# Expert gathers of six token tiles as one sequence, with layer 1's attention laid beside them

## The chip, the core and the metric

The kernel runs on one core of a Trainium2 chip, as a single launch. The metric is the device time of the launch in microseconds, as the median of several runs; lower is better. The engines are TensorE (PE, with its weight loads PEld), VectorE (DVE), ScalarE (ACT), GpSimd (POOL) and SyncE (SP). SP and POOL issue the transfers (DMA), each in a queue of its own. Engines work in parallel, each in its own order, and wait for each other with semaphores.

## What is computed

One inference step of two layers over 384 tokens (256 prompt frames and 8 streams of 16 frames), 1024 features each, all in fp32. The 384 tokens are three tiles of 128. Layer 0 is an RWKV-7 time mixing, layer 1 a differential attention; each is followed by a PEER mixer of 8 heads that picks 16 of 16384 experts per head and token. Cut to that mixer and the order of things:

```python
s = einsum('nhcd,ckd->nhck', q, sub_keys)           # q = xr @ w_query
s1, i1 = top_k(s[:, :, 0], 16); s2, i2 = top_k(s[:, :, 1], 16)
top_s, top_pos = top_k(all sums s1 + s2, 16)        # 256 candidates a head
gate = softmax(top_s); u = expert_u[eidx]
h = gelu(einsum('nhkd,nd->nhk', u, xr))
out = einsum('nhk,nhkd->nd', gate * h, expert_v[eidx])
...
x = layer_norm(DN_ALPHA * x + mix); x = layer_norm(DN_ALPHA * x + peer_ffn(x))
```

So every token needs 128 rows of expert_u and expert_v, 1 MB for each of the 128 slots of a tile of 128 tokens, 128 gathers per tile and 768 in all. Keys and values of layer 1 come from x after layer 0; the prompt's tokens see the tokens of their own and earlier chunks of 64, the sample tokens their stream's cache of 512 and their own 16.

## The kernel before

The program is a row of stages, each an `nc.Block()` at whose end all engines meet. Within a layer the stages hold all three tiles. In order: the RWKV projections, time mixing per tile, output projection and norm; `peer(0)`; `attention`; `peer(1)`; `store_rows`.

`peer` turns x to features, computes the key scores of tile 0 alone (`first_scores`) and then runs `peer_experts`. There VectorE first chooses the experts of tile 0 (`choose`, top 16 of 16 score rows and of 8 candidate rows), while TensorE and ScalarE compute the key scores of tiles 1 and 2 (`KeyScores`, weights in a ring of two 1 MB buffers). POOL then issues one gather per slot: row `expert[:, t, s]` of `in_peer_uv` for each of the 128 tokens (one per partition), 8 KB per row, u and v side by side, into a ring of ten buffers, `pair_ring`. For each gather VectorE makes the dot product of u and x (`L1386`); for two of them ScalarE applies gelu (`L1410`) and VectorE the gate (`L1392`), ScalarE writes the product on a diagonal (`L1415`), and TensorE multiplies diagonal and v into `pacc`, 128 columns of weights by two halves of 512 (`L1436`, fp32, two passes each). Its end frees the buffer (`row_used`) and lets POOL issue the gather ten further on. The choice for the next tile and the norm of the last one are laid between the dots by hand (`side`). The two layers' gathers are two separate loops of 384.

`attention` projects K, V and Q for all tiles (weights read once through `aw_ring`), turns them, runs the prompt's heads (`prompt_attention`, one step per head with both prompt tiles), the sample streams (`sample_attention`, one step per stream; the cached keys are turned on TensorE, `L1744`), the norm per head and the output projection. No gather runs there.

Of the kernel before, what the change touches and what calls it, by code (L numbers as in the profile page):

```python
# [19 lines left out]
P = 128  # L20
D = 1024
# [13 lines left out]
SLOTS = PH * PTOP  # L35
ALPHA = (2.0 * 2) ** 0.25
# [6 lines left out]
def constant_layout():  # L43

    widths = [("ident", P), ("strict_incl", 2 * P), ("lower", P), ("block", P), ("chunk", NCH), ("first", NCH),
              ("causal", 3 * P), ("pair_ident", N), ("map0", 1), ("map1", 1), ("sum_maps", DD), ("iota", PTOP), ("cos", TILES * ROT // 2),
# [8 lines left out]
def shape_constants():  # L55
# [16 lines left out]
    put("pair_ident", row % N == np.arange(N)[None, :])  # L72

# [37 lines left out]
class Core:  # L111

    def __init__(self, nc, ctx):
        self.nc, self.ctx = nc, ctx
        self.signals = {}

    def sig(self, name):
        if name not in self.signals:
            self.signals[name] = Signal(self.ctx, self.nc, name)  # L120
        return self.signals[name]

# [964 lines left out]
class KeyScores:  # L1087

    HC = 2 * PH
    PAIR = 2 * P

    def __init__(self, core, io, ctx, xT, scores, layer, tiles, ring):
        def sb(name, shape, dt=F32):
            return ctx.enter_context(core.nc.sbuf_tensor(f"{name}_{layer}_{tiles[0]}", shape, dt))

        self.core, self.io, self.xT, self.scores, self.layer, self.tiles, self.ring = core, io, xT, scores, layer, tiles, ring  # L1100
        self.rows = slice(tiles[0] * P, (tiles[-1] + 1) * P)
        self.width = len(tiles) * P
        self.wq = sb("wq", [P, ring, KD, self.PAIR])
        self.keys, self.keysT = sb("keys", [P, 2, P]), sb("keysT", [P, 2, P])
        self.qT = sb("qT", [P, self.HC, self.width])
        self.bank = [ctx.enter_context(core.nc.psum_tensor(f"pbank{i}_{layer}_{tiles[0]}", [P, HALF], F32)) for i in range(6)]
        self.wq_in = [core.sig(f"loaded{i}") for i in range(ring)]
        self.keys_in, self.keys_psum, self.keys_done = core.sig(f"loaded{ring}"), core.sig("keysT_psum"), core.sig("keys_done")
        self.q_psum, self.q_done = core.sig("rows_psum"), core.sig("rows_copied")
        self.s_psum, self.s_done = core.sig("s_psum"), core.sig("ps_done")  # L1110

    def loads(self, sp):
        sp.dma_start(self.keys[:], self.io["peer_sub_keys"][self.layer].rearrange("c k d -> k c d")).then_inc(*self.keys_in.by(16))
        for i in range(PH):
            if i >= self.ring:
                sp.wait_ge(*self.q_psum.at(2 * (i - self.ring) + 2))
# [1008 lines left out]
```

## Time and profile before

| | us |
|---|---|
| median of 3 runs | 3494.87 |
| lowest, highest | 3494.45, 3506.02 |
| the profiled execution, its own time | 3500.28 |
| its span in the trace | 3498.5 |
| TensorE, VectorE, ScalarE, POOL busy | 2615.5, 1768.4, 659.7, 946.1 |
| HBM read, written | 938.81 MB, 18.12 MB |

The profile is of one execution. Busy times are of the span, the weight loads of TensorE (1419.4 us) lie beside its products. A share of DMA is the mean over the core's 16 DMA engines. The first gather is issued at 960.69 us, layer 0's last norm is done near 1952, and layer 1's gathers run from about 2500 to 3478.5.

### The profile page before, as it was taken

To read this page: it belongs to the slowest core of one execution; us is meant where nothing else is said; L and a number is where in the kernel's file an instruction comes from. 1 tells how busy PE (TensorE), PEld (TensorE's weight loads), DVE (VectorE), ACT (ScalarE), POOL (GpSimd) and SP (SyncE) were. 2 spreads that over 40 slices of the span, in tenths; PEclk is the share of its full clock that TensorE was granted. 3 is DMA by queue.
4 is the path that set the end of the run, shared out by engine and by line. 5 is a ranking of instruction groups with operands and counts; after the bars stand their busy time and mean duration, and the time that the engine had idled before them with its cause. 6 is when DMAs were issued, how large, how long until landed. Compare 5 with 4: busy or idle time off the path is not lost. (4 is left out here: it accounts for less than half of the span.)

```text
span 3498.5 us, 32692 instructions
## 1 busy us (share of the span) xinstructions
PE 2615.5 (75%) x11853; PEld 1419.4 (41%) x11853; DVE 1768.4 (51%) x4015; ACT 659.7 (19%) x1800; POOL 946.1 (27%) x929
## 2 busy tenths in 40 slices
PE   7949494866977777777777794887877777777776
PEld 3427383753842322232222343666733222322222
DVE  1133534322558657855555204432778567755555
ACT  0022121220121211122112103311111211121112
POOL 0013130310044433444434000000144434443332
PEclk9979696987999999999999895988999999999999
DMA  5220204023599999999999412523699999999997
GB/s 176 86 107 2 73 1 100 1 44 131 164 391 420 420 420 420 403 420 420 420 420 420 160 66 120 223 103 101 242 416 412 420 420 420 407 420 420 420 420 319
DMA packets 193198, 959.04 MB, mean 274 GB/s; under 512 B 33232, under 2 KB 67200, under 8 KB 94736
## 3 DMA queue, kind: packets, MB, share of 16 engines
q0 software_dynamic: 114784, 821.12, 56.9%
q1 hardware_dynamic: 78256, 135.84, 11.6%
q8 instruction: 96, 1.57, 0.2%
q14 instruction: 62, 0.51, 0.0%
HBM read 938.81 MB, written 18.12 MB: 274 GB/s over the span
## 5 line engine op out<-in xcount | busy, mean ns | idle before, releaser
L1436 PE MATMUL pacc<-pair_ring,diag 128*128 128x512 f32 x3072 | 1439.5, 615 | 489.0 <-ACT diag L1415 488.9
L1289 POOL DMA_INDIRECT pair_ring<-in_peer_uv,expert x768 | 800.9, 1043 | 1679.4 <-PE pacc L1436 1089.6
L1386 DVE CUSTOM_DVE_ANT_0 pair_ring<-pair_ring,x_tok 128x1024 f32<-128x1024 f32 x768 | 939.5, 1225 | 622.5 <-DMA pair_ring<-in_peer_uv,expert 619.5
L1436 PEld LDWEIGHTS pacc<-pair_ring,diag 128*128 128x128 f32 x3072 | 571.2, 195 | 1356.0 <-issue 1344.6
L1410 ACT ACTIVATE acts<-dots 128x2 f32<-128x2 f32 x384 | 78.1, 203 | 1384.3 <-DVE dots L1386 1384.0
L1415 ACT ACTIVATE diag<-constants_sb,mix 128x128 f32<-128x128 f32 x768 | 266.2, 393 | 145.0 <-DVE mix L1392 143.2
L1130 PE MATMUL pbank<-peer_xT,wq 128*128 128x128 f32 (+1 forms) x1024 | 178.3, 340 | 14.0 <-DMA wq<-in_peer_w_query 14.0
L1130 PEld LDWEIGHTS pbank<-peer_xT,wq 128*128 128x128 f32 x1024 | 162.9, 201 | 29.5 <-DMA wq<-in_peer_w_query 15.3
L275 PE MATMUL acc<-w_ring,mixed 128*128 128x512 f32 x288 | 125.8, 599 | 10.0 <-issue 9.1
L1487 PE MATMUL aacc<-aw_ring,at_xT 128*128 128x512 f32 x288 | 126.4, 601 | 6.2 <-DMA aw_ring<-in_w_kv 5.6
L1392 DVE TENSOR_TENSOR mix<-gate,acts 128x2 f32<-128x2 f32 x384 | 59.6, 155 | 68.0 <-ACT acts L1410 68.0
L720 DVE TENSOR_TENSOR x<-bank,x 128x512 f32<-128x512 f32 x48 | 33.2, 692 | 116.1 <-PE bank L578 116.1
L275 PEld LDWEIGHTS acc<-w_ring,mixed 128*128 128x128 f32 x288 | 55.1, 192 | 80.0 <-issue 80.0
L1487 PEld LDWEIGHTS aacc<-aw_ring,at_xT 128*128 128x128 f32 x288 | 55.3, 193 | 76.8 <-issue 70.4
L339 DVE SCALAR_TENSOR_TENSOR mixed<-dxT,mu_cols,xT 128x384 f32<-128x384 f32 x48 | 25.8, 612 | 114.3 <-PEq L284 114.2
L517 PE MATMUL bank<-constants_sb,wkv_a 128*128 128x128 f32 x24 | 8.0, 334 | 81.9 <-PEq L382 79.9
L1195 DVE MAX8 best<-scores 128x8 f32<-128x128 f32 x96 | 21.8, 281 | 87.3 <-PEq L1160 87.3
L1386 DVE DVE_READ_ACCUMULATOR2_ANT dots<- 128x1 f32 x768 | 63.5, 83 | 0.0
L525 PE MATMUL bank<-own_ar,feat 128*128 128x256 f32 x192 | 51.8, 430 | 14.9 <-ACT own_ar L673 14.9
L769 POOL TENSOR_TENSOR B_by_chunk<-wkv_B_end,constants_sb 128x512 f32<-128x512 f32 x48 | 50.0, 1042 | 42.3 <-PE bank L610 42.2
L760 POOL MEMSET own_ar<- 128x1024 f32 x3 | 2.9, 952 | 216.2 <-POOLq L382 216.2
L416 PE MATMUL run<-wkv_z,constants_sb 128*128 128x512 f32 x12 | 11.3, 1100 | 59.3 <-DVEq L424 59.3
(372 smaller groups left out, 2639.1 us busy)
## 6 DMA issues: line engine op xcount, KB each, us to landing
wq<-in_peer_w_query SPq DMA_DIRECT2D x32, 1024.0 KB, 5.9
cache_k<-in_cache_k SPq DMA_DIRECT2D x8, 2048.0 KB, 12.2
cache_v<-in_cache_v SPq DMA_DIRECT2D x8, 2048.0 KB, 8.7
w_ring<-in_rwkv_w_rkv SPq DMA_DIRECT2D x24, 512.0 KB, 3.3
pair_ring<-in_peer_uv,expert POOLq DMA_INDIRECT x768, 18.4
aw_ring<-in_w_kv SPq DMA_DIRECT2D x16, 512.0 KB, 8.6
pn_w_rwkv<-in_rwkv_w_out SPq DMA_DIRECT2D x8, 512.0 KB, 7.1
aw_ring<-in_diff_w_q SPq DMA_DIRECT2D x8, 512.0 KB, 3.2
```

Source lines behind the costliest of these rows:

```text
L275: mm = pe.matmul(acc[:, 2 * t + h, :], xm[:, k, t * P:(t + 1) * P], w_ring[:, n % RING, h * HALF:(h + 1) * HALF], start=(k == 0), stop=(k ...
L525: mm = pe.matmul(bank[first + q][:, r * 2 * P:(r + 1) * 2 * P], feat[:, g % 2, q, n, :], own_ar[:, h].rearrange("k i t -> k (i t)"))
L720: dve.tensor_tensor(x[:, g % 2, (i + 1) % 2], quad(bank[4 + i % 2], P), x[:, g % 2, i % 2], ALU.add).then_inc(*x_done.by())
L769: pool.tensor_tensor(dst[:, h], src[:, head(g, h)].unsqueeze(1).broadcast_to([P, NCH, N]), spread, ALU.mult).then_inc(*exp_done.by())
L1130: mm = pe.matmul(self.bank[m % 3][:, 0:self.width], self.wq[:, m // 2 % self.ring, k, (m % 2) * P:(m % 2 + 1) * P], self.xT[:, k, self.row ...
L1289: pool.indirect_dma_start(ring[:, g % RING, :], None, io["peer_uv"], bass.IndirectOffsetOnAxis(ap=expert[:, t, s:s + 1], axis=0)).then_inc ...
L1386: dve.tensor_tensor_reduce(ring[:, g % RING, 0:D], ring[:, g % RING, 0:D], x[:, t, :], 1.0, 0.0, ALU.mult, ALU.add, dots[:, t % 2, s:s + 1 ...
L1392: dve.tensor_tensor(mix[:, t % 2, now], gate[:, t % 2, now], acts[:, t % 2, now], ALU.mult).then_inc(*mix_done.by())
L1410: act.activation(acts[:, t % 2, now], dots[:, t % 2, now], ACT.Gelu).then_inc(*gelu_done.by())
L1415: act.activation(diag[:, (g + j) % DIAGS, :], core.const("ident"), ACT.Copy, scale=mix[:, t % 2, i * BATCH + j:i * BATCH + j + 1]).then_in ...
L1436: mm = pe.matmul(acc[:, half, :], diag[:, g % DIAGS, :], ring[:, g % RING, D + half * HALF:D + (half + 1) * HALF], start=(s == 0), stop=(s ...
L1487: mm = pe.matmul(acc[:, b, :], xT[:, k, t * P:(t + 1) * P], ring[:, n % RING, h * HALF:(h + 1) * HALF], start=(k == 0), stop=(k == KD - 1))
```

## The change

The gathers of both layers become one sequence of 384 turns of two gathers, kept by a class `Flow` whose counters and buffers live over the whole program. A stage gets a number of ticks and the turn at which it must have arrived (`plan`), and calls `flow.vector`, `flow.scalar`, `flow.tensor` and `flow.gpsimd` after each tick of its own work; they carry the turns up to `due(n)`, TensorE and POOL one tick behind. Layer 1 is now worked through tile by tile (`attention_tile`): norm of the expert output of the tile, features, K/V/Q projection, features of K and Q, attention (tiles 0 and 1 of the prompt, tile 2 the sample streams), norm per head, output projection, features, key scores. The weights for these are read again for each tile. Its 27 stages carry turns 66 to 262, then `run_flow` and `ffn_norm` carry the rest.

A gather now serves 64 tokens, each with two of its slots: partition w and w + 64 both belong to token w. The expert numbers and gates of a tile go to DRAM and come back in that order (`turn_rows_out`, `turn_rows_in`), x is copied in it (`spread_rows`), all on POOL's queue. Two gathers j = 0, 1 serve the two halves of the tokens; each multiplies with 64 columns of weights, at columns 0 and 64 of the array. Number of gathers and their bytes stay as they were. The lambda stage (`mixing_weight`) moves ahead of the first experts, the gather buffers serve as weight ring for layer 0's key scores, and the caches come in another layout from the host, so that cached keys are no longer turned on the chip.

```diff
+class Flow:
+    RING, DIAGS = 10, 3
...
+    def due(self, n):
+        return self.first + (self.last - self.first) * n // self.ticks
...
+    def tensor(self, pe, n):
+        while self.summed < self.due(n - 1):
+            u, q = divmod(self.summed, TURNS)
+            if q == 0 and u > 0:
+                pe.wait_ge(*self.ffn_done.at(u))
+            for half in range(2):
+                for j in range(GROUPS):
+                    g = self.summed * GROUPS + j
+                    if half == 0:
+                        pe.wait_ge(*self.landed(g))
+                        pe.wait_ge(*self.diag_done.at(g + 1))
+                    mm = pe.matmul(self.acc[j * FOLD:(j + 1) * FOLD, half, :], self.diag[:, self.summed % self.DIAGS, j, :],
+                                   self.ring[:, g % self.RING, D + half * HALF:D + (half + 1) * HALF],
+                                   start=(q == 0), stop=(q == TURNS - 1), tile_position=(0, j * FOLD))
...
+    def gpsimd(self, pool, n):
...
+        while self.gathered < min(self.due(n - 1) * GROUPS + self.RING, self.known * SLOTS):
+            u, s = divmod(self.gathered, SLOTS)
+            q, j = divmod(s, GROUPS)
+            if s == 0:
+                pool.wait_ge(*self.turn_in.at(32 * GROUPS * (u + 1)))
+            if self.gathered >= self.RING:
+                pool.wait_ge(*self.row_used.at(self.gathered - self.RING + 1))
+            pool.indirect_dma_start(self.ring[:, self.gathered % self.RING, :], None, self.io["peer_uv"],
...
+    def turn_rows_out(self, pool, u):
+        pool.wait_ge(*self.soft_done.at(u + 1))
+        pool.dma_start(self.core.turn_at[u], self.expert[:]).then_inc(*self.turn_out.by(16))
+        pool.dma_start(self.core.turn_gate[u], self.gate[:]).then_inc(*self.turn_out.by(16))
+    def turn_rows_in(self, pool, u):
+        pool.wait_ge(*self.turn_out.at(32 * (u + 1)))
...
-            for s in range(SLOTS):
-                        for half in range(2):
-                            mm = pe.matmul(acc[:, half, :], diag[:, g % DIAGS, :], ring[:, g % RING, D + half * HALF:D + (half + 1) * HALF],
-                                           start=(s == 0), stop=(s == SLOTS - 1))
-                        mm.then_inc(*row_used.by())
...
-        peer(core, io, 0)
-        attention(core, io)
-        peer(core, io, 1)
-        store_rows(core, io)
...
+        open_flow(core, io, flow, xT, choice)
+        attention_tile(core, io, flow, 0, neg_lam, kT, v_tok, [
+            (69, dict(turn=((2, 0, 3),), rows=((2, 1),))), (71, {}), (86, {}), (90, {}), (102, {}), (106, {}), (115, {}), (118, {}), (130, {})])
+        attention_tile(core, io, flow, 1, neg_lam, kT, v_tok, [
+            (133, dict(rows=((3, 1),))), (135, {}), (152, dict(u=3, side=75)), (156, dict(side=20)), (168, dict(side=50, end=8)),
+            (171, dict(turn=((3, 1, 0),))), (180, dict(turn=((3, 0, 2),))), (182, {}), (194, {})])
+    attention_tile(core, io, flow, 2, neg_lam, None, None, [
+        (197, dict(rows=((4, 1),))), (199, dict(u=4, side=15)), (216, dict(side=110)), (221, dict(side=25, end=12, turn=((4, 15, 0),))), (240, dict(turn=((4, 0, 4),))),
+        (243, {}), (250, {}), (252, {}), (262, {})])
+    run_flow(core, flow, 32, 294, u=5, side=160, end=28, rows=((5, 1),), turn=((5, 31, 0),))
+    ffn_norm(core, io, flow, 3, 298)
+    run_flow(core, flow, 30, 328, turn=((5, 0, 4),))
+    ffn_norm(core, io, flow, 4, 332)
+    run_flow(core, flow, 52, 384)
+    ffn_norm(core, io, flow, 5, 384)
```

A number in the lists is the turn that the stage ends with; the nine stages of a tile are `ffn_norm`, `turn_features`, `attention_projections`, `turn_features`, the attention, `head_norm`, `project_tile`, `turn_features`, `key_scores`. `u` and `side` start a tile's choice of experts beside the stage and set its steps, `end` the tick at which it is done, `turn` the ticks of the stores and loads of expert numbers, `rows` that of the copies of x.

On POOL's queue the gathers of one layer stood in one run, with the stores of K and V behind them (before):

```order
L1289 DMA pair_ring<-in_peer_uv,expert 128x2048 x384
L1274 UNCONDITIONAL_BRANCH
L1464 UNCONDITIONAL_BRANCH
L1473 DMA out_cache_v_p<-at_v 128x2x1024
L1474 DMA out_cache_v_s<-at_v 128x1024
```

Now, around the head norm of tile 1 and the output projection behind it, the store of expert numbers stands between gathers, and its loads wait for it (after):

```order
L1373 DMA fl_pairs<-in_peer_uv,fl_row_at 128x2048 x22
L1799 UNCONDITIONAL_BRANCH
L2161 UNCONDITIONAL_BRANCH
L1380 DMA turn_at<-fl_expert 128x128
L1381 DMA turn_gate<-fl_gate 128x128
L1373 DMA fl_pairs<-in_peer_uv,fl_row_at 128x2048 x8
L2156 UNCONDITIONAL_BRANCH
L2231 UNCONDITIONAL_BRANCH
L1373 DMA fl_pairs<-in_peer_uv,fl_row_at 128x2048 x2
L1390 DMA fl_row_at<-turn_at 64x2x64 x2
L1390 DMA fl_row_gate<-turn_gate 64x2x64 x2
```

Ten gathers stand between the store and its loads; everything behind the loads on this queue waits for the store to land.

On ScalarE the heads of the prompt attention stood without any expert work between them (before; `pa_p` are the probabilities):

```order
L1637 ACTIVATE pa_p,pa_tot<-pa_s,pa_low 128x128
L1637 ACTIVATE pa_p,pa_tot<-pa_s,pa_low 128x256
L1637 ACTIVATE pa_p,pa_tot<-pa_s,pa_low 128x128
L1637 ACTIVATE pa_p,pa_tot<-pa_s,pa_low 128x256
L1626 COPY pa_attnT<-pa_t 128x384
L1628 COPY at_oT<-pa_o 128x256
```

Now one tick of the stage of tile 0 reads (after; the functions Exp and Gelu lie in different tables):

```order
L1845 ACT_TABLE_LOAD
L1845 ACTIVATE pa_p,pa_tot<-pa_s,pa_low 128x128 x2
L1850 COPY pa_attnT<-pa_t 128x128
L1852 COPY at_oT<-pa_o 128x128
L1317 ACTIVATE fl_diag<-constants_sb,fl_mix 128x64 x2
L1325 ACT_TABLE_LOAD
L1325 ACTIVATE fl_acts<-fl_dots 128x2
```

A diagonal, a gelu and two table loads stand in each head's step.

## Rows read from the trace of the kernel before

In rows of engines' busy time the columns are the stretch, its length, then busy us (and instructions) of PE, PEld, DVE, ACT and POOL, the granted TensorE clock as a share of full speed, the DMA share, and GB/s. Rows in order of time begin with start and duration in us.

**Rows 1.** The page, part 2: the span in 40 slices.

```profile
PEclk9979696987999999999999895988999999999999
DMA  5220204023599999999999412523699999999997
GB/s 176 86 107 2 73 1 100 1 44 131 164 391 420 420 420 420 403 420 420 420 420 420 160 66 120 223 103 101 242 416 412 420 420 420 407 420 420 420 420 319
```

**Rows 2.** Busy time (and instructions) of each engine by stretch.

```profile
960.00:1930.00 970.00, 724.63 (x1626) 296.47 (x1625) 605.89 (x1392) 191.61 (x597) 399.93 (x384) 0.98 1.01 416
...
1957.00:2100.00 143.00, 132.38 (x317) 61.06 (x318) 8.21 (x16) 12.49 (x23) 2.59 (x4) 0.95 0.30 110
...
2108.00:2180.00 72.00, 32.67 (x143) 23.10 (x144) 32.93 (x113) 22.05 (x81) 1.51 (x1) 0.55 0.36 146
2180.00:2320.00 140.00, 120.45 (x1259) 92.63 (x1257) 56.67 (x146) 40.76 (x113) 2.04 (x2) 0.94 0.44 166
2320.00:2345.00 25.00, 18.08 (x96) 17.80 (x96) 13.37 (x39) 1.15 (x2) 0.00 (x0) 0.64 0.08 25
...
2403.00:2447.00 44.00, 36.15 (x290) 35.41 (x290) 0.21 (x2) 6.99 (x21) 0.00 (x0) 0.88 0.62 194
```

**Rows 3.** The same view between the end of one tile and the next.

```profile
1298.79:1623.10 324.31, 240.04 (x512) 95.23 (x512) 220.94 (x537) 63.94 (x200) 137.84 (x128) 0.97 1.01 415
1623.10:1944.24 321.14, 237.88 (x512) 93.33 (x512) 171.40 (x327) 61.05 (x196) 120.17 (x119) 0.99 0.98 406
```

**Rows 4.** The page, part 5: the expert groups.

```profile
L1436 PE MATMUL pacc<-pair_ring,diag 128*128 128x512 f32 x3072 | 1439.5, 615 | 489.0 <-ACT diag L1415 488.9
L1289 POOL DMA_INDIRECT pair_ring<-in_peer_uv,expert x768 | 800.9, 1043 | 1679.4 <-PE pacc L1436 1089.6
L1386 DVE CUSTOM_DVE_ANT_0 pair_ring<-pair_ring,x_tok 128x1024 f32<-128x1024 f32 x768 | 939.5, 1225 | 622.5 <-DMA pair_ring<-in_peer_uv,expert 619.5
```

**Rows 5.** PE in order of time: 64-column stationaries, then 128.

```profile
276.08 1.94 PE L600 MATMUL bank<-B_by_chunk,x 128*64 128x512 f32 x8
...
1019.37 3.67 PE L1436 MATMUL pacc<-pair_ring,diag 128*128 128x512 f32 x8 [1.31 <-ACT diag L1415]
```

**Rows 6.** DMA queues in 20 to 22 us: packets, MB, share of time.

```profile
q1 hardware_dynamic: 108, 0.42, 52.9%
q0 software_dynamic: 111, 0.41, 50.7%
```

**Rows 7.** Queue q1 in 1963:2033, 2108:2320, 2345:2352 and 2403:2447.

```profile
q1 hardware_dynamic: 3312, 12.06, 48.0%
...
q1 hardware_dynamic: 8448, 33.56, 41.3%
...
q1 hardware_dynamic: 752, 2.74, 98.3%
...
q1 hardware_dynamic: 8592, 8.52, 62.0%
```

**Rows 8.** Start of the expert stage in order of time.

```profile
960.69 1.06 POOL L1289 DMA_INDIRECT pair_ring<-in_peer_uv,expert  x1 [239.68 <-DVEq L1323]
...
980.94 1.28 ACT L1402 ACT_TABLE_LOAD   x1
982.23 0.31 ACT L1402 ACTIVATE gate<-gate 128x128 f32<-128x128 f32 x1
...
983.13 0.29 DVE L1334 TENSOR_TENSOR gate<-gate,norm 128x128 f32<-128x128 f32 x1
```

**Rows 9.** The lambda stage in order of time.

```profile
1952.61 0.33 SPq L1532 DMA_DIRECT2D lam_rows<-in_diff_lambda  x1
...
1956.61 0.15 DVE L1548 TENSOR_SCALAR at_neg_lam<-at_neg_lam 128x1 f32<-128x1 f32 x1
```

**Rows 10.** The last rows of the chain of waits.

```profile
3459.78 18.72 DMA pair_ring<-in_peer_uv,expert
...
3491.12 1.22 DVE x_tok L1353
```

More of the change, by code:

```diff
@@ L35 @@
 SLOTS = PH * PTOP
+GROUPS = 2
+FOLD = P // GROUPS
+TURNS = SLOTS // GROUPS
 ALPHA = (2.0 * 2) ** 0.25
@@ L1178, in drain, with advance @@
         pass
+def advance(part, n):
+    for _ in range(n):
+        if next(part, part) is part:
+            return
 def settle(eng, ins, steps):
@@ new lines, in first_scores, with _ @@
+def first_scores(core, io, flow, xT, scores):
+    with ExitStack() as ctx:
+        part = KeyScores(core, io, ctx, xT, [scores], 0, (0,), 4, "first", wq=flow.ring[:, 0:4].rearrange("p r (k n) -> p r k n", k=KD))
+        with core.nc.Block() as block:
+            @block.sync
+            def _(sp):
+                part.loads(sp)
+            @block.tensor
+            def _(pe):
+                part.products(pe)
+            @block.scalar
+            def _(act):
+                part.copies(act)
+        core.end_stage()
@@ new lines, in run_flow, with _ @@
+def run_flow(core, flow, ticks, last, **events):
+    flow.plan(ticks, last, **events)
+    with core.nc.Block() as block:
+        @block.gpsimd
+        def _(pool):
+            for n in range(1, ticks + 1):
+                flow.gpsimd(pool, n)
+        @block.tensor
+        def _(pe):
+            for n in range(1, ticks + 1):
+                flow.tensor(pe, n)
+        @block.scalar
+        def _(act):
+            for n in range(1, ticks + 1):
+                flow.scalar(act, n)
+        @block.vector
+        def _(dve):
+            for n in range(1, ticks + 1):
+                flow.vector(dve, n)
+    core.end_stage()
@@ L1504, in _ @@
+                for n in range(1, 3 * KD + 1):
+                    if n > KD and n % KD in (1, 2):
+                        copy_half(act, n // KD - 1, n % KD - 1)
+                    flow.scalar(act, n)
+                copy_half(act, 2, 0)
+                copy_half(act, 2, 1)
+                flow.scalar(act, TICKS - 1)
+                flow.scalar(act, TICKS)
             @block.vector
@@ new lines, in key_scores, with _ @@
+def key_scores(core, io, flow, xT, choice, t, last, **events):
+    with ExitStack() as ctx:
+        part = KeyScores(core, io, ctx, xT, [choice.scores[:, 0]], 1, (0,), 2, f"late{t}")
+        flow.plan(part.ticks, last, **events)
+        with core.nc.Block() as block:
+            @block.sync
+            def _(sp):
+                part.loads(sp)
+            @block.gpsimd
+            def _(pool):
+                for n in range(1, part.ticks + 1):
+                    flow.gpsimd(pool, n)
+            @block.tensor
+            def _(pe):
+                part.products(pe, flow)
+            @block.scalar
+            def _(act):
+                part.copies(act, flow)
+            @block.vector
+            def _(dve):
+                for n in range(1, part.ticks + 1):
+                    flow.vector(dve, n)
```

1614 lines of the change are left out of this document (907 added, 707 removed).

## The prediction, made before the changed kernel ran

> **What bounds the kernel now.** First read the slices of the page [rows 1]. In two blocks of ten slices the transfers stand at 9 with 400 to 420 GB/s. These are the expert stages of the two layers. Between them lie seven slices at 60 to 266 GB/s, the attention of layer 1, where the core's DMA engines mostly idle. Then read the same by stretch [rows 2]. In the first expert stage the DMA share is 1.01 and TensorE is busy 725 of 970 us, VectorE 606. In the attention stretches the share is 0.30, 0.36 and 0.44 and TensorE does the work (132 of 143 us, 120 of 140). So two different resources bound two kinds of stage, and they never work at the same time. From the end of one tile to the next, 128 gathers take 321.14 us, 2.51 us each, and 324.31 us where a choice of experts runs beside them [rows 3]. The groups agree: a gather is issued in 1.04 us and VectorE's dot product takes 1.22 us, both below 2.51; VectorE's idle time of 622 us is ended by the gathers [rows 4]. The chain of waits ends in 18.7 us gather pieces [rows 10].
>
> **What the change does, part by part.** I build the new span as one sum: the time at which gathers start, all the bytes that must move afterwards at the rates of the rows, the tail, and what stays idle.
>
> *Start.* Before, the first gather is issued at 960.69, before the softmax of tile 0, and ScalarE comes to the exponent only after all copies of key scores; the softmax ends at 983.4 [rows 8]. Now a gather needs expert numbers that went through DRAM, and POOL sends them only after the softmax. The lambda stage, some 5 us from load to last result [rows 9], also moves ahead of it: 988.4. Then come two stores of POOL, their landing, four loads and the four copies of rows issued behind them. No row has just this; a POOL issue is about 1 us [rows 4] and I estimate 10 us for both round trips (4 to 20 are the bounds), so issue at about 998. For the descriptors I add an estimate of 3 us (in the first two stretches of two us behind the issue at 960.69 the gathers' queue moved nothing yet); hence 1001.
>
> *Gathers.* 768 at 2.509 us is 1927 us, if never starved.
>
> *Other bytes beside them.* K, V and query weights: 48.0% of 70 us is 33.6 us for 12.06 MB, so 35 us for 12.6 MB. They are now read for each tile: 105. Cache: 41.3% of 212 us, 88. Query weights of the experts' layer 1: 62.0% of 44 us, 27.3, three times: 82. Output weights with the two rows of the norm: 98.3% of 7 us for 2.74 MB, 2.51 us per MB. At this rate 15.7 MB of them, 5.2 MB for five other norms, 4.2 MB of spread rows, and 4.1 MB of stores come to 73, with 7 for the small turns of expert numbers: 80 [rows 7]. Together 355.
>
> *Tail.* The last gather lands at 3478.5, the span ends at 3498.5 [rows 10]: 20. The last norm is now a stage of its own, with its rows loaded after a barrier, and a storing stage behind it: 25.
>
> Sum without idling: 1001 + 1927 + 355 + 25 = 3308.
>
> *Do the engines keep up?* TensorE multiplies with 64 columns of weights, two gathers in the two halves of the array. The nearest rows are exact in shape: eight passes of 128x64 by 512 columns, in alternating halves, take 1.94 us, where eight with 128 columns take 3.67 [rows 5]. A turn of two gathers thus costs TensorE 1.94 of 5.02 us. VectorE needs 171.4/64 = 2.7 us per turn, and a choice of experts 221 - 171 = 50 us [rows 3]. The attention part spans turns 66 to 262, 196 turns. Its DMA time is 984 plus some 340 of the other bytes, 1324. TensorE needs 196 x 1.94 + about 460 for attention and key scores (the busy times of [rows 2], key scores three times) = 840, VectorE 196 x 2.7 + three choices + 132 = 810. Both fit with a third to spare. The removed turning of cached keys is not on the new bound and brings nothing more. In the stage that opens the flow, two choices fall on 56 turns: 2.7 + 100/56 = 4.5 of 5.02 us, just covered.
>
> *What stays idle.* An in-order engine now stands between the stage's work and the flow, and ten gathers in the ring cover 25 us. I count: (a) Key scores. Queues share by packets when both are full: 108 against 111 [rows 6]. The DMA engines are busy in that time, and only the restart is idle: about 4 us, three times, 12. (b) Prompt attention took 72 us for eight heads, 9 us per head, with TensorE busy 33 and VectorE 33: a chain. A stage of one tile has ten ticks and 12 turns, 60 us of gathers. ScalarE loads its table twice per tick, 1.28 us each [rows 8]. I take 7.5 us per tick, between 6 (hidden) and 9, so 15 us lost, twice: 30. (c) Turning expert numbers, five times after the first. The store stands in POOL's queue behind the gathers of the ring, and POOL issues nothing while it waits for it. When it lands the queue ahead is empty. Two latencies and four issues, about 8 us, less what was issued between: 5 times 5, 25. (d) Cached attention: 88 + 95 = 183 us of bytes against 140 us before plus nineteen turns: 10. (e) Some 30 barriers, each mostly covered by the ring: 20. Together 97; the bounds are 20 and 190. Span 3405.
>
> The profiled execution took 3500.3 for a span of 3498.5, and the median of the runs is 3494.9, 5.4 lower. So 3405 + 1.8 - 5.4 = 3401; I say 3400, a gain of 2.7%.
>
> **Rules weighed.** The rows on the two queues show equal numbers of packets at two full queues. The Trainium skill, page "DMA: Bandwidth & Descriptors", section "Queues, rings and completion order", says the same: each DMA engine goes round its queues packet by packet. By this rule, the trace agrees, small packets lose against gathers. Were it a split by bytes, the first load would land in 5 us and term (a) would be 0, with a span of 3393.
>
> **Rivals.**
> *Nearly perfect overlap* (chance 0.15): idle under 35 us, 3310 to 3340. For it speaks the spare third on each engine. Against it stands the chain of prompt attention.
> *The clock makes TensorE the bound* (0.07). Where TensorE was busy 45% and 72% of a stretch, the granted clock was 0.55 and 0.64, and 0.94 at 86% [rows 2]: at 0.5 it is the 1.2 GHz level. Now a turn fills 39% of TensorE's time. At half clock throughout, the attention part would need 2 x 840 = 1680 against 1324, a loss of 356. Since a full engine was granted 0.94 to 0.98, half of that is the more likely price: 3401 + 178 = 3580. The expert part alone, at 3.9 of 5.02 us, would stay hidden.
> The Trainium skill, page "TensorE: Matmul & The Clock Gate", section "HAM oscillation — how this bites in real kernels", says that waits for transfers between short bursts throw the clock to its lower level. By it the flow in the last 122 turns would run at half clock and cost nothing.
> *Waiting does not overlap, it adds* (0.13, the other side). Each tick has VectorE and TensorE wait for a landed gather, and only then does the head or batch behind it start; if its chain is longer than the tick's gathers, the ring fills and the DMA engines stop. Price: the stretch from the end of layer 0's gathers to 2500 is some 556 us. If half of it stays outside the gathers, the idle time is 278 instead of 97: 3582. It decides from 191 us of idle on (97 and the 94 of the forecast gain), 7 us for each of the 27 attention stages.
> *Partial form of it* (0.10): 150 to 200 us idle, 3450 to 3510.
> *Forecast* (0.55): 3340 to 3450.
>
> **How the numbers follow.** What a measurement of this kernel can tell from no change is about 0.5%, 17 us, so 3477 and 3512 are the limits. Faster takes the forecast, perfect overlap, and half of the partial form, with a little of the two others, where they come weakly: 0.78. Same: 0.08. Slower: 0.14. The range of eight in ten reaches from 3320 to 3500; it leaves out the lower end of perfect overlap and the full form of the two slow rivals. The forecast's own range is 3340 to 3450.
>
> **What the profile would show.** DMA share at 0.9 or more in the slices from about 1000 us to the end, with 390 GB/s or more; the first gather near 998; the flow's passes in groups of eight at about 1.9 us (3.9 where the clock is low); 768 gathers, 2.5 us apart in the last 122 turns; TensorE's longest waits at the start of the key score stages, for query weights, above 20 us; prompt attention near 75 us a tile. The attention part ends (turn 262) near 1001 + 262 x 5.02 + 340 + 80 = 2740. Wrong would be a share below 0.85 between 1350 and 2700, a first gather after 1010, or POOL waiting over 10 us for each turning of expert numbers. Then the idle terms are too small, in that order of price.

## The result and the profile after

The changed kernel takes 3824.0 us (median of 4, 3816.82 to 3829.81), the kernel before it 3499.2 in the same comparison (4 runs, 3494.45 to 3506.02): ratio 1.0926, 95% interval 1.0896 to 1.0955. It is 9.3% slower where 2.7% faster was forecast. (A span is up to 2 us shorter than the time of its execution.) The profiled execution has a span of 3822.4 us, 417 more than the 3405 of the forecast.

First the page of the changed kernel: span, slices, queues, and the groups that answer to [rows 1] and [rows 4].

```profile
span 3822.4 us, 33101 instructions
PE 2256.5 (59%) x11771; PEld 1243.4 (33%) x11771; DVE 1749.3 (46%) x4053; ACT 675.7 (18%) x1897; POOL 1040.6 (27%) x985
...
PEclk9978787888877769676878667787787788776877
DMA  5210103045699979787779677778876789899998
GB/s 172 100 67 7 61 13 80 2 127 157 242 420 392 396 276 401 275 337 288 280 280 385 228 279 306 281 297 339 328 319 268 284 296 419 351 366 375 373 420 339
...
q0 software_dynamic: 117024, 825.84, 54.5%
q1 hardware_dynamic: 95104, 187.39, 14.0%
...
L1349 PE MATMUL fl_acc<-fl_pairs,fl_diag 128*64 128x512 f32 x3072 | 1069.0, 789 | 793.8 <-ACT fl_diag L1317 793.5
L1373 POOL DMA_INDIRECT fl_pairs<-in_peer_uv,fl_row_at x768 | 864.3, 1125 | 1822.1 <-PE fl_acc L1349 1691.3
L1296 DVE CUSTOM_DVE_ANT_0 fl_pairs<-fl_pairs,fl_rows 128x1024 f32<-128x1024 f32 x768 | 923.6, 1223 | 408.4 <-DMA fl_pairs<-in_peer_uv,fl_row_at 407.9
```

The seven empty slices of [rows 1] are gone, but the full blocks on both sides of them are gone too: from the fifteenth to the thirty-second slice the DMA row reads mostly 7 and 8. No engine is full. Each waits for another: POOL for TensorE (1691 us), TensorE for ScalarE's diagonals (794), VectorE for gathers (408). Such a ring of waits says that something all share keeps stopping them, not what it is. By stretch (columns: engines' busy time with instructions, granted clock, DMA share, GB/s) it reads:

```profile
1003.00:3822.40 2819.40, 1534.80 (x5578) 707.45 (x5578) 1402.48 (x3409) 496.51 (x1564) 893.94 (x817) 0.76 0.84 332
...
1374.10:3166.00 1791.90, 1004.28 (x4120) 493.02 (x4122) 771.48 (x1878) 334.62 (x997) 454.48 (x436) 0.76 0.78 302
1408.30:1431.00 22.70, 9.49 (x24) 3.98 (x24) 5.98 (x14) 2.42 (x10) 5.07 (x4) 0.58 0.52 185
1431.00:1546.20 115.20, 79.09 (x216) 25.59 (x216) 41.07 (x87) 14.62 (x51) 30.66 (x30) 0.87 0.95 383
1787.60:1911.20 123.60, 70.03 (x386) 51.73 (x386) 29.46 (x60) 14.97 (x58) 23.67 (x24) 0.79 0.73 273
```

The first line is everything behind the first gather: 16% of 2819 us idle, 451 us, where the forecast had 97 and a tail of 25. The second is the attention part, 1792 us for 196 turns and an idle share of 22%, 394 us. The third is one of its shortest stages, the turn of tile 0 to features: two turns of gathers, 10 us of transfers, take 22.7 us with the DMA engines idle half of it, although TensorE works 9.5 and VectorE 6.0 us. The projection stage (fourth line) is full at 0.95; the key score stage (fifth) is not.

What happens in the short stage is seen at the end of the stage ahead of it. These are rows of the changed kernel's timeline (start, duration, engine, line, operation, idle time before it and its releaser) and then two-microsecond stretches of the same place.

```profile
1392.58 2.00 PE L1349 MATMUL fl_acc<-fl_pairs,fl_diag 128*64 128x512 f32 x8
1393.80 0.20 ACT L1325 ACTIVATE fl_acts<-fl_dots 128x2 f32<-128x2 f32 x1 [1.70 <-DVE fl_dots L1296]
1397.48 0.94 POOL L1373 DMA_INDIRECT fl_pairs<-in_peer_uv,fl_row_at  x1 [0.30 <-issue]
1408.32 0.16 DVE L1286 TENSOR_TENSOR fl_mix<-fl_row_gate,fl_acts 128x2 f32<-128x2 f32 x1 [14.56 <-PEq L1601]
1408.32 0.45 PE L1672 MATMUL tn_at_x<-constants_sb,x_tok 128*128 128x128 f32 x1 [13.74 <-PEq L1601]
1409.46 3.73 PE L1349 MATMUL fl_acc<-fl_pairs,fl_diag 128*64 128x512 f32 x8 [0.69 <-ACT fl_diag L1317]
1413.35 0.94 POOL L1373 DMA_INDIRECT fl_pairs<-in_peer_uv,fl_row_at  x1 [14.92 <-PE fl_acc L1349]
```

```profile
1396.00:1398.00 2.00, 0.00 (x0) 0.00 (x0) 0.00 (x0) 0.00 (x0) 1.46 (x2) 1.00 0.92 348
1398.00:1400.00 2.00, 0.00 (x0) 0.00 (x0) 0.00 (x0) 0.00 (x0) 0.43 (x1) 0.82 1.01 418
1400.00:1402.00 2.00, 0.00 (x0) 0.00 (x0) 0.00 (x0) 0.00 (x0) 0.00 (x0) 0.50 0.99 418
...
1404.00:1406.00 2.00, 0.00 (x0) 0.00 (x0) 0.00 (x0) 0.00 (x0) 0.00 (x0) 0.50 0.95 401
1406.00:1408.00 2.00, 0.00 (x0) 0.00 (x0) 0.00 (x0) 0.00 (x0) 0.00 (x0) 0.50 0.03 12
1408.00:1410.00 2.00, 0.99 (x3) 0.70 (x5) 0.16 (x1) 0.75 (x3) 0.00 (x0) 0.50 0.00 0
1410.00:1412.00 2.00, 2.00 (x6) 0.92 (x4) 0.00 (x0) 0.00 (x0) 0.00 (x0) 0.50 0.00 0
1412.00:1414.00 2.00, 1.78 (x8) 0.42 (x4) 0.51 (x3) 0.27 (x1) 0.65 (x1) 0.77 0.00 0
1414.00:1416.00 2.00, 0.00 (x0) 0.00 (x0) 2.00 (x4) 0.00 (x0) 1.64 (x2) 1.00 0.46 94
```

The last product of the stage ends at 1394.6. TensorE and VectorE start again at 1408.3, just after the transfers have gone to zero at about 1406. Nothing moves for 8 us, until TensorE has used a turn (3.73 us at the low clock, where the turn ahead of the boundary took 2.00) and POOL may issue again at 1413.35. The profile puts the wait down to TensorE's queue at L1601, the line of the stage's block. Asking for the instructions of that line, with the queues' own instructions, names the real one (count: shortest, median, longest in ns, first and last start). One row each for the eight forms of attention stage from 1374 to 3166, then the stages with gathers alone:

```profile
L1601 POOLq DRAIN  x3: 11796/13412/13417, 1394.6 to 2490.3; - x3
L1654 POOLq DRAIN  x9: 8237/9046/10474, 1421.2 to 3031.2; - x9
L1710 POOLq DRAIN  x3: 16178/17463/18282, 1528.5 to 2635.5; - x3
L1799 POOLq DRAIN  x2: 11945/14996/18047, 1637.6 to 2219.5; - x2
L1953 POOLq DRAIN  x1: 11112/11112/11112, 2920.6 to 2920.6; - x1
L2156 POOLq DRAIN  x3: 12247/12382/12953, 1677.0 to 2953.3; - x3
L2223 POOLq DRAIN  x3: 10395/15486/15729, 1741.4 to 3007.4; - x3
L2277 POOLq DRAIN  x3: 10892/11092/11320, 1899.6 to 3135.4; - x3
...
L1564 POOLq DRAIN  x3: 21512/23727/24476, 3298.7 to 3782.0; - x3
```

### The profile page after: what moved, and what is told of

It is laid out like the page before. It is cut to its first block and busy times, and to the rows that moved or that the text cites. A ratio compares the mean times of both kernels' runs of the same rounds, so it can differ in the third digit from the quotient of the medians.

```text
span 3822.4 us, 33101 instructions
## 1 busy us (share of the span) xinstructions
PE 2256.5 (59%) x11771; PEld 1243.4 (33%) x11771; DVE 1749.3 (46%) x4053; ACT 675.7 (18%) x1897; POOL 1040.6 (27%) x985
## 5 line engine op out<-in xcount | busy, mean ns | idle before, releaser
L1349 PE MATMUL fl_acc<-fl_pairs,fl_diag 128*64 128x512 f32 x3072 | 1069.0, 789 | 793.8 <-ACT fl_diag L1317 793.5
L1373 POOL DMA_INDIRECT fl_pairs<-in_peer_uv,fl_row_at x768 | 864.3, 1125 | 1822.1 <-PE fl_acc L1349 1691.3
L1296 DVE CUSTOM_DVE_ANT_0 fl_pairs<-fl_pairs,fl_rows 128x1024 f32<-128x1024 f32 x768 | 923.6, 1223 | 408.4 <-DMA fl_pairs<-in_peer_uv,fl_row_at 407.9
L1349 PEld LDWEIGHTS fl_acc<-fl_pairs,fl_diag 128*64 128x64 f32 x3072 | 418.5, 170 | 1350.6 <-issue 1274.2
L1286 DVE TENSOR_TENSOR fl_mix<-fl_row_gate,fl_acts 128x2 f32<-128x2 f32 x384 | 59.1, 155 | 647.5 <-ACT fl_acts L1325 284.6
L1317 ACT ACTIVATE fl_diag<-constants_sb,fl_mix 128x64 f32<-128x64 f32 x768 | 224.6, 341 | 590.7 <-DVE fl_mix L1286 556.6
L1325 ACT ACTIVATE fl_acts<-fl_dots 128x2 f32<-128x2 f32 x384 | 78.1, 203 | 1022.9 <-DVE fl_dots L1296 1022.5
L1446 PE MATMUL pbank_late<-at_yT,wq_late 128*128 128x128 f32 x768 | 113.1, 312 | 74.3 <-DMA wq_late<-in_peer_w_query 74.1
L1446 PEld LDWEIGHTS pbank_late<-at_yT,wq_late 128*128 128x128 f32 x768 | 105.4, 222 | 100.8 <-DMA wq_late<-in_peer_w_query 78.9
L1296 DVE DVE_READ_ACCUMULATOR2_ANT fl_dots<- 128x1 f32 x768 | 63.3, 82 | 0.0
```

Of the source, the lines that this page charges most:

```text
L1286: dve.tensor_tensor(self.mix[:, u % 2, q, :], self.row_gate[:, u % TILES, :, q], self.acts[:, u % 2, q, :], ALU.mult).then_inc(*self.mix_d ...
L1296: dve.tensor_tensor_reduce(pair, pair, self.rows[:, u % 2, j, :], 1.0, 0.0, ALU.mult, ALU.add, self.dots[:, u % 2, q, j:j + 1]).then_inc(* ...
L1317: act.activation(self.diag[:, self.diagged % self.DIAGS, j, :], self.core.const("fold_ident"), ACT.Copy, scale=self.mix[:, u % 2, q, j:j + ...
L1325: act.activation(self.acts[:, u % 2, q, :], self.dots[:, u % 2, q, :], ACT.Gelu).then_inc(*self.gelu_done.by())
L1349: mm = pe.matmul(self.acc[j * FOLD:(j + 1) * FOLD, half, :], self.diag[:, self.summed % self.DIAGS, j, :], self.ring[:, g % self.RING, D + ...
L1373: pool.indirect_dma_start(self.ring[:, self.gathered % self.RING, :], None, self.io["peer_uv"], bass.IndirectOffsetOnAxis(ap=self.row_at[: ...
```

## Experiments

Each kernel was compared with the kernel before on the same chip (there 3506 to 3508 us, where the comparison of the result had 3499.2). One run each unless an interval is given; the four runs of experiment 5 spread over 15 us, so single runs that lie closer than that are not told apart. Differences between kernels are plain differences of the times. The expectations set theories against each other: A, chains of waits of in-order engines within a stage; B, turns and stages disturb each other; C, TensorE at the low clock; D, bytes; E, the DRAIN; F, the gather ring and a weight ring that wait in turns for the one in-order TensorE.

**1. No turns beside the attention stages.** The same 27 stages with constant turn numbers; 64, 64 and 68 turns in stages of their own.

```
-            (69, dict(turn=((2, 0, 3),), rows=((2, 1),))), (71, {}), (86, {}), ...
+            (66, dict(turn=((2, 0, 3),), rows=((2, 1),))), (66, {}), (66, {}), ...
+        run_flow(core, flow, 64, 130)
```

> The changed kernel with no gather laid beside layer 1's attention: the 27 attention stages are the same and stay in their order, but take no turns; the 64 turns that each tile waits for run in a stage of their own between the tiles (66 to 130, 130 to 194, 194 to 262). It measures what the attention stages take by themselves (B) in this piecewise form. The 196 turns take 984 us alone (5.02 each); laid beside each other the two took about 1790 us (1374 to 3166). Theory A (the in-order stages and the turns mostly add up; the stages of one tile are long by themselves): B is about 1000 us, so the time is about 3822 - 1790 + 984 + 1000 = 4016, and laying them beside each other saved only some 200 of 984. Theory B (the stages alone are about as long as the 490 us of before, and the turns beside them are what makes them long): B is 500 to 600, the time about 3550, below the changed kernel. Between them, 3822, the overlap is worth nothing.

Measured 3818.17 us, against 3824.0: within the noise the overlap is worth nothing. The layer norms start at 1377.3, 1902.4, 2465.6 and 3316.7; less 64, 64 and 100 turns of 5.02 us, the stages alone take 204, 242 and 349, together B = 795 us. Neither number was right: B lies between the theories, above the 556 us that nearly the same work took before ([rows 3] to the gathers at 2500) and below 1000. The table gives tile 0 from the starts of the stages in the timelines: alone, laid beside its turns, and beside them without the DRAIN (experiment 5).

| stage | turns | alone | changed kernel | no DRAIN |
|---|---|---|---|---|
| layer norm | 3 | 18.6 | 34.2 | 25.6 |
| x to features | 2 | 2.6 | 22.7 | 13.0 |
| K, V, Q | 15 | 51.6 | 115.2 | 105.8 |
| k, q to features | 4 | 4.2 | 38.0 | 30.8 |
| prompt attention | 12 | 25.0 | 71.8 | 63.2 |
| head norm | 4 | 13.7 | 33.6 | 25.2 |
| output projection | 9 | 26.7 | 67.7 | 59.0 |
| y to features | 3 | 2.6 | 30.3 | 20.6 |
| key scores | 12 | 50.7 | 123.6 | 113.2 |
| sum | 64 | 196 | 537 | 456 |

196 us of stages and 321 of turns one after the other are 517; beside each other they took 537.

**2. Half of TensorE's passes per turn.**

```
-            for half in range(2):
+            for half in range(1):
```

> The changed kernel with four TensorE passes for a turn of gathers in place of eight: the second 512 columns of the experts' output are left out (the first stand in for them). Transfers and VectorE are unchanged. If the low clock makes TensorE's turns the cost (theory C), four passes save 1.0 us at the high and 1.9 at the low clock in each of 196 turns of the attention part, 200 to 370 us, and the time falls to 3450 to 3620. If the waits of the in-order stages set it (theory A), the turn is only one link of them: 50 to 150 us, 3670 to 3770. If transfers set it: no change.

Measured 3735.69, 88 us less: inside theory A's span, far from theory C's. The span's mean clock even fell, from 0.782 to 0.69, while the time fell.

**3. A short dot product.**

```
-                dve.tensor_tensor_reduce(pair, pair, self.rows[:, u % 2, j, :], ...
+                dve.tensor_tensor_reduce(pair[:, 0:P], pair[:, 0:P], self.rows[:, u % 2, j, 0:P], ...
```

> The changed kernel with VectorE's dot product over 128 of 1024 features, the rest of the sum left out: 1.2 us becomes about 0.25, 1.9 us less per turn. Theory A: VectorE's dot stands ahead of the stage's own steps on an in-order engine and in the loop gather, dot, gate, diagonal, product, so it is on the path in part of the turns: 100 to 250 us less, 3570 to 3720. Theory C (TensorE's clock) and transfers as the bound: under 50 us.

Measured 3759.32, 65 us less; below what A wanted, above C. VectorE's group shrank from 923.6 to 209.8 us, so 714 us of work taken away gave 65. Neither TensorE's nor VectorE's work on the turns is the main cost; ScalarE's was not tested.

**4. Half the bytes.**

```
-            pool.indirect_dma_start(self.ring[:, self.gathered % self.RING, :], None, ...
+            pool.indirect_dma_start(self.ring[:, self.gathered % self.RING, 0:D], None, ...
-    put("peer_uv", np.concatenate([... for n in ("peer_u", "peer_v")], 1))
+    put("peer_uv", np.asarray(inputs["peer_u"]).reshape(-1, D))
```

> The changed kernel with gathers of 4 KB rows in place of 8 KB (only the first weight vector of an expert is read, and used for both): half the bytes of every gather, engines' work unchanged. The stages with gathers alone (turns 0 to 66 and 262 to 384) fall from 5.0 us per turn to some 3.5 to 4, as TensorE and the issue allow: about 200 us less. In the attention part the transfers fall from about 1400 to 910 us. Theory A (chains of waits, not bytes): the part stays above 1500 us, the total is about 3400. If bytes and queue order set the part (theory D), it falls by 400 or more and the total is below 3200.

Measured 3302.97. Its attention part, in one stretch, and the DRAINs at the ends of its key score stages:

```profile
1285.20:2865.00 1579.80, 996.88 (x4154) 486.94 (x4154) 784.24 (x1946) 338.02 (x1010) 472.31 (x445) 0.78 0.63 215
```

```profile
L2277 POOLq DRAIN  x3: 7262/7366/7617, 1733.3 to 2821.7; - x3
```

1580 us at a DMA share of 0.63: theory A's "above 1500". The part fell by 212 us, far from theory D's 400. The total is 100 lower than I expected, since the stages with gathers alone gave some 300 us, not 200: the last 122 turns with the tail took 436 us, where the changed kernel has 656, and the first 66 took 288 for 371. With half the bytes in flight the DRAIN is shorter too at this boundary, 7.4 for 11.1 us.

**5. Stages closed without GpSimd's DRAIN.** In the 11 forms of stage:

```
-    with core.nc.Block() as block:
+    with core.nc.Block(no_gpsimd_drain=True) as block:
```

> The changed kernel with its 11 forms of stage (32 boundaries) closed by a barrier that leaves out GpSimd's DRAIN, nothing else. In the changed kernel's trace the DRAIN of GpSimd at the end of a stage lasts until the last gather in flight has landed: 13.4 us at 1394.6, 327 us in the 27 boundaries from 1374 to 3166, 424 in all from 1370 on; every other engine stands at the barrier meanwhile, and at its end no transfer is under way (whole gaps of 155 us beside the boundaries of the attention part). Theory E (the drain of the gather ring at each boundary is where the overlap went): the gaps go and the engines' waits shrink, 155 to 330 us less, 3490 to 3670, with the short stages (2 turns in about 22 to 30 us) at 10 to 15 us. Theory A (chains of in-order waits within the stages): under 60 us less, since the same waits come at the next tick: 3760 or more.

Measured 3543.28 us (3539.77 to 3554.36), ratio to before 1.0114, 1.0095 to 1.0133. One keyword gives back 281 us, within theory E's span. Each gather still has its own semaphore, on which its readers wait (`landed`), and the DRAINs of the other engines stay. The windows of this kernel: everything from 1003 on, the attention part, key scores of tile 0, prompt attention of tile 1, cached attention, and the last 56 turns.

```profile
1003.00:3538.00 2535.00, 1518.38 (x5578) 703.19 (x5578) 1407.29 (x3409) 496.96 (x1564) 887.04 (x816) 0.79 0.92 369
...
1351.40:2915.00 1563.60, 985.69 (x4114) 490.23 (x4114) 768.40 (x1860) 334.30 (x994) 450.92 (x437) 0.80 0.89 348
1694.60:1807.80 113.20, 71.29 (x386) 53.00 (x386) 29.47 (x60) 14.88 (x58) 21.92 (x23) 0.80 0.78 295
1994.00:2081.00 87.00, 52.44 (x168) 24.71 (x168) 76.96 (x182) 45.06 (x101) 25.50 (x21) 0.71 0.63 233
2500.20:2717.80 217.60, 145.94 (x1160) 89.09 (x1160) 80.14 (x216) 57.51 (x153) 40.21 (x44) 0.80 0.86 337
3230.00:3519.00 289.00, 166.20 (x456) 66.27 (x456) 154.92 (x293) 47.64 (x174) 122.06 (x108) 0.79 1.00 414
```

As many instructions of the engines as before, to within a few, with a share of 0.92 where it was 0.84, and 1564 us for the attention part where it was 1792. In its timeline POOL issues gathers across the boundary at 1377.0 (1375.81, 1377.10, 1378.36, 1380.20).

**6. Experiment 1 without the DRAIN.**

> The kernel of the first experiment (no turns beside the attention stages, 64 in a stage of their own between the tiles), which took 3818, with the same barriers without the DRAIN. Its attention stages have no gather in flight except at some ten boundaries, where the DRAIN takes 12 to 23 us. Theory E: only those boundaries gain, about 8 us each: 3720 to 3770, so that the laid-beside kernel without DRAIN is now below it by 100 us or more. Theory A: both stay where they were, equal within 30 us.

Measured 3727.91. The same sum as for experiment 1 gives 190, 234 and 329, together 753 us for the stages alone. It is 90 less than experiment 1, some 9 us for each of its some ten boundaries with gathers in flight, and now 185 above experiment 5. Without the DRAIN the overlap is worth 185 us.

**7. The last 52 turns in 13 stages.**

```
-    run_flow(core, flow, 52, 384)
+    for last in range(336, 385, 4):
+        run_flow(core, flow, 4, last)
```

> The changed kernel with its last stage of 52 turns cut into 13 stages of 4 turns: 12 more boundaries with the DRAIN, where nothing but gathers is done. The price of a boundary by itself. Theory E: each drains the ring and refills it, 6 to 12 us: 72 to 144 us more, 3895 to 3970. Theory A: a boundary is a barrier of about 1 to 2 us, and the ring of ten gathers covers it: at most 25 us more.

Measured 3933.99, 110 more for 12 boundaries: 9.2 us each, with nothing but gathers in these stages (8.6 if each kernel is first set against the kernel before on its own chip).

```profile
L1564 POOLq DRAIN  x15: 52/18652/23173, 3294.6 to 3905.1; - x15
```

A DRAIN is 18.7 us here (median) and costs 9.2: while it waits the last gathers still move bytes. The cost is the standstill until the next can be issued and land; at the boundary shown above, 1.7 us of it is TensorE's turn at the low clock, which released POOL's next issue.

**8. The kernel before without the DRAIN.** In 8 forms of stage.

> The kernel before the change with the barriers without DRAIN in its stages behind layer 0's attention-like part (8 forms). It has two boundaries with gathers in flight, whose DRAIN took 21.9 us each, at the ends of the two expert stages; nothing can be issued behind them there but the next stage's loads. Theory E and A alike: 0 to 15 us less, 3480 to 3500.

Measured 3506.36 against 3506.09, ratio 1.0003 (0.9993 to 1.0012). As expected nothing: its two long DRAINs stand where no gather could follow, and the first ends at 1941.2 while VectorE works on the norm until 1952.1. They are in the trace of before, at the line of the expert stage:

```profile
L1274 POOLq DRAIN  x2: 21909/21918/21926, 1919.3 to 3459.6; - x2
```

**9. Larger rings for late query weights**, on the kernel of experiment 5.

```
-        part = KeyScores(core, io, ctx, xT, [choice.scores[:, 0]], 1, (0,), 2, f"late{t}")
+        part = KeyScores(core, io, ctx, xT, [choice.scores[:, 0]], 1, (0,), 3 if t < 2 else 5, f"late{t}")
```

> The kernel without the DRAIN (3543) with room for three blocks of query weights in the key score stages of tiles 0 and 1 and five in that of tile 2, in place of two. In those stages TensorE waits for the weights 23 us in four waits of up to 10, the twelve turns stand behind it, and the DMA engines then stand idle while the ring is full and landed: 25, 25 and 16 us of idle transfer time, the largest left. Theory F (the two small rings take turns waiting for the one in-order engine): 30 to 60 us less, 3485 to 3515. Rival: the idle time moves to the next wait and the gain is under 10 us.

Measured 3492.49 (3480.99 to 3497.17), ratio to before 0.9955 (0.9936 to 0.9974): 51 less. TensorE's group of late query weights in experiment 5, then here:

```profile
L1446 PE MATMUL pbank_late<-at_yT,wq_late 128*128 128x128 f32 x768 | 116.5, 318 | 60.3 <-DMA wq_late<-in_peer_w_query 60.3
```

```profile
L1446 PE MATMUL pbank_late<-at_yT,wq_late 128*128 128x128 f32 x768 | 102.0, 294 | 26.1 <-DMA wq_late<-in_peer_w_query 26.1
```

The key score stage of tile 0 went from 113 to 95 us. Theory F's 30 to 60 holds.

**10. Half the passes, on the kernel of experiment 5.**

> The kernel without the DRAIN (3543) with four TensorE passes per turn in place of eight (the second 512 columns of the experts' output are left out), as in the second experiment, where this brought 88 us. Theory C (clock and TensorE's turns are part of what is left): 60 us or more less, under 3480. Otherwise, with the ring kept filled over the boundaries, the turn's passes lie beside transfers: 0 to 30 us less, 3513 to 3543.

Measured 3478.52, 65 less, just past the bound of 60 that I had set for theory C (one run, and the bound lies within its noise): part of the turn's passes is on the path even so. The mean clock was 0.704, lower than the 0.806 of experiment 5. Whether a higher clock would give part of it was not tried.

**11. 35 of 50 steps of the choice moved out of prompt attention**, on the kernel of experiment 9.

```
-(152, dict(u=3, side=75)), (156, dict(side=20)), (168, dict(side=50, end=8))
+(152, dict(u=3, side=110)), (156, dict(side=20)), (168, dict(side=15, end=8))
```

> The kernel with the larger rings of query weights, and of the 50 steps of choosing experts that stood in the ten ticks of tile 1's prompt attention 35 moved to the projection stage ahead of it. TensorE waits there 20 us for VectorE's attention steps, behind the steps of the choice, and the DMA engines idle 32 of 87 us; the projection stage is full (idle under 1 us, 112 us long, VectorE busy half of it). Theory F: 15 to 25 us less than with the larger rings alone. Rival: the attention chain of that stage is as long by itself, under 5 us.

Measured 3484.05 (3472.72 to 3495.93), ratio to before 0.9925 (0.9904 to 0.9946). That is 0.75% below the kernel before, outside the noise but small. It is 8 us below experiment 9, short of theory F's 15 to 25, and the intervals do not tell the two apart. Between the layer norms of tiles 1 and 2 lie 460.6 us, where experiment 9 has 471.3; but between those of tiles 0 and 1, where the two kernels do not differ, lie 448.6 and 439.3. Whether the choice's place costs anything stays open.

**12. The 13 stages of experiment 7, without the DRAIN.**

> The last stage of 52 turns cut into 13 stages of 4, as in the experiment that cost 110 us more, now on the kernel without the DRAIN (3543). If the DRAIN was the price of a boundary (9.2 us each with it), the 12 boundaries now cost 0 to 2 us each: 3543 to 3567. If the price is that of meeting at a barrier whatever closes it, they cost 6 us or more each: 3615 or more.

Measured 3553.84, 10.6 above experiment 5: 0.9 us per boundary, a difference that lies within the spread of experiment 5's own runs, so it may be less. So the DRAIN was the price, not the barrier.

## Why the prediction was wrong

The span was missed by 417 us. Step by step:

*Start.* The first gather was issued at 1003.5, not 998. From the first store (996.1) to this issue lie 7.5 us, for an estimate of 10; the softmax ended at 995.7, 7 us later than forecast. Right to 5 us.

*Engines.* A turn takes TensorE 1.94 to 2.14 us at the high clock and up to 3.9 at the low one, 2.78 in the mean (1069.0 us by 384), where [rows 5] gave 1.94. "Both fit with a third to spare" held as a sum of busy times, and was the wrong question: experiments 2 and 3 took hundreds of microseconds of work away for 88 and 65.

*Bytes.* Behind the first gather 0.84 of 2819 us are busy, 2368, for a forecast of 2282. The forecast is 86 us too low; 36 of them went with the DRAIN (0.92 of 2535 is 2332). A share has two digits, so each of these busy times is good to 14 us only. The other 326 us of the miss are idle time and tail: 451, for a forecast of 125 (97, the tail of 25 and 3 for the descriptors).

*(e) Some 30 barriers, "each mostly covered by the ring", 20 us.* This is the step that failed. The ring does not cover a boundary; the boundary empties the ring. A boundary cost 9.2 us in experiment 7, 0.9 without the DRAIN, and leaving the DRAIN out at all 33 boundaries with gathers in flight (27 in the attention part, 6 outside) gave 281 us, 8.5 each. I had the number of boundaries and a cover, and never asked how a stage is closed. The trace of before had the answer: 21.9 us of DRAIN at each end of the expert stage, between POOL's last issue and the barrier. It cost nothing there (experiment 8), and the views of waits do not name it. Of the miss of 417 us, 261 are this term, 281 for 20.

*(a) Key scores, 12 us.* TensorE's first product with query weights comes 7 us after the start of the stage (1787.6 to 1794.5 in the timeline), not 23: the stage begins behind a drained ring. In experiment 5 gathers are in flight there, and it comes 12 us after the start (1694.6 to 1706.5). For two microseconds (1698.6 to 1700.6) the queues moved 110 packets of gathers and 109 of weights, equal numbers as the prediction has it; in the two microseconds ahead and behind, as the one queue began and the other ran out, they moved 114 and 20, then 75 and 326. But only 3 MB of gathers were still to move, not a full ring, and so the 23 us were too many. And I took only the restart as idle. With two rings that both wait for an in-order TensorE, transfers and TensorE stood still in turns. Four stretches of the changed kernel's stage show it (TensorE works and the transfers all but stand, then the reverse, then both once more; the two last columns are DMA share and GB/s):

```profile
1795.60:1799.60 4.00, 3.31 (x16) 2.94 (x17) 0.00 (x0) 0.75 (x3) 0.00 (x0) 0.62 0.04 13
1811.60:1815.60 4.00, 0.00 (x0) 0.00 (x0) 1.01 (x2) 0.00 (x0) 0.00 (x0) 0.58 1.04 426
1823.60:1827.60 4.00, 4.00 (x22) 2.33 (x18) 0.98 (x2) 0.00 (x0) 1.46 (x2) 0.71 0.12 16
1839.60:1843.60 4.00, 0.00 (x0) 0.00 (x0) 0.00 (x0) 0.00 (x0) 0.00 (x0) 0.50 1.03 413
```

TensorE waited for query weights four times in this stage, 30 us in all. Larger weight rings gave back 51 us. The in-order engine between stage and flow was named, the size was four times too small.

*(b) Prompt attention, 30 us.* It took 72 us for tile 0 (forecast 75), near 100 for tile 1, where steps of the choice stood ahead of the attention's. Both times contain the DRAIN at the stage's end. Without it they are 63 and 87, and tile 1's stage still idled 37% of 87 us, 32 us. So the length of 75 was met for tile 0 by luck, and the term was too small for tile 1; that the choice is the reason was not shown (experiment 11).

*(c) Turning expert numbers, 25 us.* At the five later turnings of the changed kernel POOL's loads are issued right behind a gather, with no wait for the store; only the very first, which is no part of this term, shows one, 1.6 us. The stores had landed in time. Too large.

*(d) Cached attention, 10 us.* 217.6 us at 0.86 without the DRAIN, 30 idle. Too small.

*Rivals.* "Waiting adds" was given 3582 and 0.13. Its observation was right (experiment 1: the overlap was worth nothing), but the price of 7 us per stage was put on chains of waits within a stage. Without the DRAIN the kernel takes 3543; how much of that is such waits is not known, and that it lies near 3582 is luck. The clock rival did not occur: TensorE was busy 1004 of the 1792 us of the attention part and so did not bound it. (Experiments 2 and 10 had a lower clock and a shorter time, but with half of the turns' passes, so they do not price the clock.) In the last 122 turns, around 3600, the groups of passes alternate between 2.1 and 3.4 to 3.8 us while gathers stay 2.5 us apart. The Trainium skill, page "TensorE: Matmul & The Clock Gate", section "HAM oscillation — how this bites in real kernels", says that waits between short bursts throw the clock to the lower level. The trace agrees for every second group, and there it cost nothing, since the transfers were at a share of 1.01 (3600 to 3640).

*A term that was not there.* The stages by themselves take longer in the new form: 795 us (experiment 1) for 556 before. I put this down to weights that are read three times and to narrow stages; no run separates the two. I had entered the bytes, 105 and 82, but not the chains. Under a full overlap this would cost nothing; with the overlap of experiment 5, in which a turn cost 4.1 us ((1564 - 753)/196, with the 753 us of the stages alone in experiment 6) for 5.02, I take it to be why even that kernel only comes to 1% above before.

Accounted, each beyond what the forecast had entered: 261 of 417 us by the DRAIN (281 for 20) and 39 by the weights' rings (51 for 12). Of the remaining 117 some 50 are transfers beyond the forecast and 5 the later start; how the rest divides between prompt attention, cached attention, TensorE's passes and the tail was not settled. Of the prediction's own signs of being wrong the first came: a share of 0.78 from 1374 to 3166, where it named 0.85. The attention part ended at 3166 for 2740.

## What to carry to other kernels

When work is pipelined across stages, look up how a stage is closed before counting on a prefetch: on the engine that issues the gathers, list its queue's own instructions at the line of the block. Here the ring in flight did not cover such a boundary, it lengthened it. And a stall that costs nothing where it stands becomes a price per boundary when the change multiplies the boundaries: 2 here became 33.

An overlap is tested quickest by taking it out: the same stages with no turns beside them gave 3818 for 3824, which no view of busy shares would have told. Where two rings feed one in-order engine, ask whether each is deep enough to bridge the time in which the engine waits for the other, not only its own transfer.

## What the runs showed of the hardware

GpSimd's DRAIN behind indirect transfers lasted 8.2 to 24.5 us in the changed kernel, until the last of them had landed, and 7.4 for 11.1 us at the same boundary where the rows had half the bytes. A boundary with it cost 9.2 us (experiment 7), without it 0.9 us (experiment 12). TensorE's clock fell during it: after the last product at 1394.6 it was granted 1.00 until 1398 and 0.50, the 1.2 GHz level, from 1400 to 1412, and it was at 1.00 again at 1414, after 4.8 us of products since 1408. Over the attention part the granted clock was 0.76 with the DRAIN and 0.80 without it.
